# A transformer pass on one core: each feed-forward network computed in three parts, each part followed by its share of the down projection

## The chip, the cores and the metric

The kernel runs on one core of a Trainium2 chip, whose other cores are idle. The metric is the time of one execution in device microseconds. TensorE multiplies, VectorE (DVE), ScalarE (ACT) and GpSimd (POOL) work on whole tiles of 128 partitions by 512 elements, and SyncE (SP) issues the transfers from HBM. Every engine runs its own program in order, and a semaphore is what makes one wait for another.

## What is computed

One sequence of 512 tokens of width 1024 passes through a mixer block, a memory attention, two more mixers and five feed-forward networks (FFN 0 to 4), each with 2816 hidden channels. The change concerns the five networks. In the reference they are these two functions (the first is FFN 0, the second FFN 1 to 4), and the lines around FFN 0:

```python
def conv_ffn(n, w_up, conv_w, conv_b, w_down):
    u, g = jnp.split(n @ w_up, 2, axis=-1)
    ...
    gc = sum(gp[:, j:j + S] * conv_w[j] for j in range(CONV_WIDTH)) + conv_b
    return (jax.nn.silu(gc) * u) @ w_down
...
def swiglu(x, w_gate, w_up, w_down):
    return (jax.nn.silu(x @ w_gate) * (x @ w_up)) @ w_down
...
        n = rms_norm(h, norm_ffn[l])
        h = h + conv_ffn(n, w_up[l], conv_w[l], conv_b[l], w_down[l])
    return rms_norm(h, final_norm)
```

After FFN 0 the residual is normed twice in a row: `final_norm` ends the first block, and the norm of FFN 1 follows at once.

## The kernel before

**Data.** The residual `h` lies transposed in SBUF as 8 tiles (`KT`) of 128 channels by 512 tokens. All matrix products are in three passes: an operand is split in a rounded part and a rest (`_hi` and `_lo`, type fp32r), and `products` (L1793 to L1795) adds w_hi·x_hi, w_hi·x_lo and w_lo·x_hi into one PSUM bank.

**Weights.** They come from HBM as one stream of 248 chunks of 1 MB, in the order of use. A chunk goes to one of two `stage` buffers by a transfer on SP's queue; ACT makes `w_hi` of it (`split_hi`, L450), DVE `w_lo` (`split_lo`, L901), each in one of two buffers. `split_hi` of a chunk waits until PE has finished the chunk two before (`chunk_done`); PE waits for `lo_ready`. A chunk holds 8 k-tiles by 2 output tiles, so 48 products of 128x512; the two output tiles take 2 of 4 PSUM banks, which alternate, so the next but one chunk needs them evacuated (`acc_evac`).

**An FFN** has two stages. `up` has 22 chunks, in pairs: a gate chunk and an up chunk, each of 2 of the 22 hidden tiles. DVE evacuates the gate (L947; for FFN 0 followed by the convolution), ACT takes the SiLU, DVE evacuates the up product (L964), POOL multiplies them (L1672), ACT rounds the result into `f_hi` (L497), DVE writes the rest `f_lo` (L968). All 22 tiles are kept: `f_hi` and `f_lo` hold 22 tiles each. `down` has 12 chunks: for each of 4 pairs of output tiles the 22 hidden tiles in chunks of 8, 8 and 6, which accumulate in the same two PSUM banks. The third chunk of each three is padded in HBM, and PE works 36 products on it.

**The residual** stage (`residual`) belongs to the end of each `down`: per pair of output tiles DVE adds the PSUM banks to `h` (L926), then splits the next chunk's weights (L901), and writes `x_lo` of the two tiles (L932) behind ACT's `x_hi` (L469). POOL follows with `sums`: per tile it squares `h` into `sq` (L1648) and adds that to `ssum` (L1650). PE sums `ssum` over the partitions by a product with ones (`stat`, L1833) after the first chunk of the next stage, ACT takes the root, DVE the reciprocal, and that `rstd` is needed for the evacuation of that first chunk.

**After FFN 0** a second sum is formed for the double norm: ACT writes the weighted squares to `sq_b` (L473), POOL adds them to `both_sum`, which lies in `up_b` (L1656), for both tiles of a pair, and only then does it square and sum the two tiles as above. PE's product with `both_sum` (`both`, L1838) stands after the first chunk of FFN 1's `up` stage. The plain sum is used for `final_norm` itself: PE's `stat(3)` stands after all of `up` of FFN 1, then ACT and DVE make the factor, and POOL multiplies the 8 tiles of `h` by the gain (L1720) and by the factor (L1724) before the down projection is added.

In all these stages the loops are hardware loops (`walk`), with two chunks, or the chunks of two pairs of output tiles, in a turn.

Of the kernel before, what the change touches and what calls it, by code (L numbers as in the profile page):

```python
# [19 lines left out]
F32 = mybir.dt.float32  # L20
# [28 lines left out]

PHASES = [  # L50
    ("qf", 6, 12), ("v", 2, 4), ("gla", 12, 24), ("kv_a", 1, 2), ("merge", 4, 16), ("mix_out", 4, 8),
    ("mem_k", 4, 8), ("mem_v", 4, 8), ("mem_q", 4, 8), ("mem_o", 4, 8),
    ("up0", 22, 44), ("down0", 12, 8),
    ("up1", 22, 44), ("down1", 12, 8),
    ("a_in", 5, 10), ("mla", 3, 20), ("a_out", 4, 8),
    ("up2", 22, 44), ("down2", 12, 8),
    ("up3", 22, 44), ("down3", 12, 8),
    ("c_in", 12, 24), ("c_out", 4, 8),
    ("up4", 22, 44), ("down4", 12, 8),
# [57 lines left out]
def build(nc, stream, x_in, mem_in, pos_in, par_in, const_in, out):  # L117
    ctx = ExitStack()
    with ctx:
# [42 lines left out]
        f_hi = place("f_hi", HID, [P, FT, S], F32R)  # L162
        f_lo = place("f_lo", hid(FT), [P, FT, S], F32R)
# [103 lines left out]
        def sem(name):  # L267
# [24 lines left out]
        qf_act, f_ready1, g_ready = sem("qf_act"), sem("f_ready1"), sem("g_ready")  # L292
# [4 lines left out]
        const_landed, wa_const_ready, kv_done, rot_step = (  # L297
            sem("const_landed"), sem("wa_const_ready"), sem("kv_done"), sem("rot_step"))
# [8 lines left out]
        mem_landed, mem_sq_ready, mem_stat, mem_std, mem_n, mem_hi_ready, mem_ready = (  # L307
            sem("mem_landed"), sem("mem_sq_ready"), sem("mem_stat"), sem("mem_std"), sem("mem_n"), sem("mem_hi_ready"), sem("mem_ready"))
# [6 lines left out]
        rope2_landed, lat_sq, lat_stat, lat_std, lat_recip, lat_n, lat_hi_ready, lat_ready = (  # L315
            sem("rope2_landed"), sem("lat_sq"), sem("lat_stat"), sem("lat_std"), sem("lat_recip"), sem("lat_n"), sem("lat_hi_ready"), sem("lat_ready"))
        pool_scaled = sem("pool_scaled")
        u_pad, pool_step, pl_hi_ready, pl_ready, mla_tile, cat0_hi, cat0_ready = (
            sem("u_pad"), sem("pool_step"), sem("pl_hi_ready"), sem("pl_ready"), sem("mla_tile"), sem("cat0_hi"), sem("cat0_ready"))
        mla_const, t5_ready, kr_sum, kr_copied = sem("mla_const"), sem("t5_ready"), sem("kr_sum"), sem("kr_copied")  # L320
# [7 lines left out]
        cu_pad, cu_ready, cv_step, cz_ready, cc_hi_ready, cc_ready = (  # L328
            sem("cu_pad"), sem("cu_ready"), sem("cv_step"), sem("cz_ready"), sem("cc_hi_ready"), sem("cc_ready"))
# [10 lines left out]
        UPS = {f"up{i}": i for i in range(5)}  # L340
# [6 lines left out]
        for name in RESIDUALS:  # L347
            XR0[name] = KT + _n
            _n += KT if FOLLOWED[name] else 0

# [88 lines left out]
        def _(act):  # L439
# [16 lines left out]
            def residual(name):  # L456
                r0, t0, c0 = XR0[name], T0[name], C0[name]
                gain = FOLLOWED[name]
                per = 6 if name.startswith("down") else 2

                def step(it):
                    for pair in range(2):
                        for k in range(per // 2):
                            split_hi((c0 + 2 + pair * (per // 2) + k, it * per))
# [17 lines left out]
            def up(name):  # L482
                c0, t0, f0, conv = C0[name], T0[name], FT * UPS[name], name == "up0"

                def step(it):
                    split_hi((c0 + 2, it * 2))
                    for e in range(2):
                        if conv:
                            act.wait_ge(conv_step, it * 6 + 3 * e + 3)
                            act.activation(gate_b[:, e, 1:1 + S], up_b[:, e, :], ACT.Silu).then_inc(silu_ready, 1)  # L490
                        else:
                            act.wait_ge(acc_evac, it * 4 + t0 + e + 1)
                            act.activation(gate_b[:, e, 1:1 + S], gate_b[:, e, 1:1 + S], ACT.Silu).then_inc(silu_ready, 1)
                    split_hi((c0 + 3, it * 2))
                    for e in range(2):
                        act.wait_ge(prod_ready, it * 2 + f0 + e + 1)
                        act.activation(row(f_hi, it * 2 + e), up_b[:, e, :], ACT.Copy).then_inc(f_hi_ready, 1)  # L497
# [2114 lines left out]
```

## Time and profile before

| what | value |
|---|---|
| time, median of 3 runs | 2785.27 us (2784.6 to 2785.38) |
| the profiled execution, from first to last instruction | 2783.7 us |
| PE busy | 2765.9 us, 99% |
| PE weight load busy | 2293.1 us, 82% |
| DVE, ACT, POOL busy | 1427.2, 1006.1, 509.2 us (51%, 36%, 18%) |
| granted TensorE clock | 1.000 over the span |
| mean DMA rate | 95 GB/s |

The page gives the profiled execution by its span alone, 2783.7 us; what a run's time has beside it is the 1.6 us by which the median is higher. Busy time of PE is an account of records that overlap: a product is shown 0.39 us long, and the next starts before it has ended, so the distance from start to start is what tells how fast PE works.

### The profile page before, as it was taken

The page shows a single profiled execution, that of the slowest core. Times are in us where ns is not written, and L with a number is a line of the kernel's source. Part 1 is how long each engine was busy: PE and PEld are TensorE (multiplying, and loading weights), DVE is VectorE, ACT ScalarE, POOL GpSimd, SP SyncE. Part 2 cuts the span into 40 slices and gives each one's busy share as a digit, 9 for nine tenths or more (in the row PEclk, how much of TensorE's full clock was granted, in tenths as well). Part 3 has the DMA queues.
Part 4 walks back from the last instruction along what each step waited for, and adds up shares of the span by engine and source line. Part 5 has one row for each costly group of instructions (what it writes and reads, how often), then busy time and mean ns, then how long its engine had stood idle before and what let it go on. Part 6 is the DMA issues. An engine that isn't in the chain of part 4 may idle for free.

```text
span 2783.7 us, 33669 instructions
## 1 busy us (share of the span) xinstructions
PE 2765.9 (99%) x12836; PEld 2293.1 (82%) x12836; DVE 1427.2 (51%) x1392; ACT 1006.1 (36%) x1099; POOL 509.2 (18%) x364
## 2 busy tenths in 40 slices
PE   9999999999999999999999999999999999999999
PEld 7978889878888888888778888888888888888887
DVE  5778766566654444343575444334443455644422
ACT  4333633434432344332263444324443222344421
POOL 0124013041101310052123100121110222501100
PEclk9999999999999999999999999999999999999999
DMA  4212024223222322323212222232223322232232
GB/s 165 90 62 79 31 106 148 79 76 106 91 105 95 115 92 90 105 91 105 99 35 74 104 91 97 99 106 104 92 90 106 106 98 99 91 105 91 90 106 91
DMA packets 39676, 264.97 MB, mean 95 GB/s; under 512 B 4528, under 2 KB 5808, under 8 KB 8240
## 3 DMA queue, kind: packets, MB, share of 16 engines
q1 hardware_dynamic: 38016, 259.02, 26.8%
q10 hardware_dynamic: 1584, 4.87, 0.5%
q8 instruction: 56, 0.92, 0.1%
q14 instruction: 20, 0.16, 0.0%
HBM read 261.77 MB, written 2.10 MB: 95 GB/s over the span
## 4 chain that ended last, share of the span: by engine, by line
PE 96%; DVE 2%; ACT 1%; issue 0%; DMA 0%; SPq 0%; POOL 0%; DVEq 0%; POOLq 0%; ACTq 0%
PE ps L1793 30%; PE ps L1794 30%; PE ps L1795 30%; PE ps L1956 1%; PE ps L2022 1%; PE ps L2053 1%; PE ps L2347 1%; PE ps L2319 1%; PE ps L1978 1%; DVE w_lo L901 0%; PE ps L2036 0%; PE ps L2331 0%; ACT w_hi L450 0%; DMA stage<-in_stream 0%; PE ps L1833 0%
## 5 line engine op out<-in xcount | busy, mean ns | idle before, releaser
L450 ACT ACTIVATE w_hi<-stage 128x2048 fp32r<-128x2048 f32 x241 | 462.8, 1920 | 1354.3 <-PE ps L1795 1351.8
L1793 PE MATMUL ps<-x_hi,w_hi 128*128 128x512 f32 x2400 | 943.3, 393 | 2.2 <-DVE w_lo L977 2.0
L1795 PE MATMUL ps<-x_hi,w_lo 128*128 128x512 f32 x2400 | 934.0, 389 | 0.0
L1794 PE MATMUL ps<-x_lo,w_hi 128*128 128x512 f32 x2400 | 933.9, 389 | 0.0
L901 DVE TENSOR_TENSOR w_lo<-stage,w_hi 128x2048 fp32r<-128x2048 f32 x241 | 602.1, 2498 | 397.1 <-ACT w_hi L450 397.1
L1793 PEld LDWEIGHTS ps<-x_hi,w_hi 128*128 128x128 f32 x2400 | 450.6, 188 | 98.9 <-issue 3.5
L1794 PEld LDWEIGHTS ps<-x_lo,w_hi 128*128 128x128 f32 x2400 | 450.7, 188 | 95.4 <-issue 3.4
L1795 PEld LDWEIGHTS ps<-x_hi,w_lo 128*128 128x128 f32 x2400 | 450.5, 188 | 93.9
L1793 PE MATMUL ps<-f_hi,w_hi 128*128 128x512 f32 x880 | 342.7, 389 | 0.0
L1794 PE MATMUL ps<-f_lo,w_hi 128*128 128x512 f32 x880 | 342.3, 389 | 0.0
L1795 PE MATMUL ps<-f_hi,w_lo 128*128 128x512 f32 x880 | 342.3, 389 | 0.0
L1672 POOL TENSOR_TENSOR up_b<-up_b,gate_b 128x512 f32<-128x512 f32 x110 | 118.1, 1094 | 1050.9 <-DVE up_b L964 1034.8
L964 DVE TENSOR_TENSOR up_b<-ps,rstd 128x512 f32<-128x512 f32 x110 | 71.0, 687 | 299.1 <-PE ps L1795 299.0
L1793 PEld LDWEIGHTS ps<-f_hi,w_hi 128*128 128x128 f32 x880 | 165.2, 188 | 34.7 <-issue 0.2
L1795 PEld LDWEIGHTS ps<-f_hi,w_lo 128*128 128x128 f32 x880 | 165.2, 188 | 34.3
L1794 PEld LDWEIGHTS ps<-f_lo,w_hi 128*128 128x128 f32 x880 | 165.2, 188 | 34.3 <-issue 0.2
L947 DVE TENSOR_TENSOR gate_b<-ps,rstd 128x512 f32<-128x512 f32 x110 | 71.0, 688 | 230.2 <-PE ps L1795 229.2
L1648 POOL TENSOR_TENSOR sq<-h 128x512 f32 x64 | 80.6, 1259 | 500.1 <-DVE h L926 494.1
L1650 POOL TENSOR_TENSOR ssum<-ssum,sq 128x512 f32<-128x512 f32 x64 | 140.0, 2187 | 5.0
L926 DVE SCALAR_TENSOR_TENSOR h<-ps,h 128x512 f32 (+1 forms) x72 | 46.4, 686 | 131.2 <-PE ps L1795 127.1
L932 DVE SCALAR_TENSOR_TENSOR x_lo<-h,par,x_hi x64 | 104.2, 1666 | 0.0
L497 ACT ACTIVATE f_hi<-up_b 128x512 f32 x110 | 69.8, 635 | 26.7 <-POOL up_b L1672 23.1
(401 smaller groups left out, 2616.3 us busy)
## 6 DMA issues: line engine op xcount, KB each, us to landing
stage<-in_stream SPq DMA_DIRECT2D x242, 1024.0 KB, 4.9
h<-in_x ACTq DMA_DIRECT2D x2, 1024.0 KB, 5.7
out_x<-h SPq DMA_DIRECT2D x8, 256.0 KB, 6.0
h<-in_x SPq DMA_DIRECT2D x6, 256.0 KB, 4.4
mem_raw<-in_mem ACTq DMA_DIRECT2D x1, 1024.0 KB, 4.8
stage<-in_stream SPq DMA_DIRECT2D x6, 128.0 KB, 5.0
h<-in_x SPq DMA_DIRECT2D x1, 512.0 KB, 5.4
mask_f<-in_constants ACTq DMA_DIRECT2D x1, 448.0 KB, 6.3
```

The source lines that it names most:

```text
L450: act.activation(w_hi[slot][:, :], stage[slot][:, :], ACT.Copy).then_inc(hi_ready, 1)
L497: act.activation(row(f_hi, it * 2 + e), up_b[:, e, :], ACT.Copy).then_inc(f_hi_ready, 1)
L901: dve.tensor_tensor(w_lo[slot][:, :], stage[slot][:, :], w_hi[slot][:, :].bitcast(F32), ALU.subtract).then_inc(lo_ready, 1)
L932: dve.scalar_tensor_tensor(row(x_lo, it * 4 + m), row(h, it * 4 + m), pc(gain, it * 4 + m), row(x_hi, it * 4 + m).bitcast(F32), ALU.mult, ...
L947: dve.tensor_tensor(gate_b[:, e, 1:1 + S], ps[:, (t0 + e) % 4, :], rstd[:, :], ALU.mult).then_inc(acc_evac, 1)
L964: dve.tensor_tensor(up_b[:, e, :], ps[:, (t0 + 2 + e) % 4, :], rstd[:, :], ALU.mult).then_inc(acc_evac, 1)
L1648: pool.tensor_tensor(sq[:, :], row(h, m), row(h, m), ALU.mult).then_inc(sq_ready, 1)
L1650: pool.tensor_tensor(ssum[:, :], ssum[:, :], sq[:, :], ALU.add).then_inc(ss_ready, 1)
L1672: pool.tensor_tensor(up_b[:, e, :], up_b[:, e, :], gate_b[:, e, 1:1 + S], ALU.mult).then_inc(prod_ready, 1)
L1793: pe.matmul(out_ap, wh, xh, start=first, stop=False)
L1794: pe.matmul(out_ap, wh, xl, start=False, stop=False)
L1795: return pe.matmul(out_ap, wl, xh, start=False, stop=last)
```

## The change

Each FFN is cut in three parts: hidden tiles 0 to 7, 8 to 15 and 16 to 21 (`PARTS`: 4, 4 and 3 pairs of up chunks). After the up chunks of a part come 4 down chunks, one for each pair of output tiles, with 8, 8 or 6 k-tiles. Each down chunk now ends in an evacuation: for parts a and b DVE adds it to `h` straight away, and part c is followed by the `residual` stage as before, now with one chunk to a pair of output tiles. `f_hi` and `f_lo` shrink to 8 tiles each. The chunks stay 248 and the products as many; the padded chunks stand together at the end. Up stages and the down stages are written out instead of looped. For FFN 1, `h` has to be scaled before the first part is added: `stat(3)`, the root, the reciprocal and POOL's 16 instructions move into the second, third and fourth step of the up stage. Some semaphores are merged to save their number; these waits are the same in meaning.

```diff
+KP = KT // 2
+PARTS = [("a", 0, 4), ("b", 4, 4), ("c", 8, 3)]
+STEPS = FT // 2
...
-        f_hi = place("f_hi", HID, [P, FT, S], F32R)
-        f_lo = place("f_lo", hid(FT), [P, FT, S], F32R)
+        f_hi = place("f_hi", HID, [P, 8, S], F32R)
+        f_lo = place("f_lo", hid(8), [P, 8, S], F32R)
...
# vector engine, residual stage (per is now 2 everywhere)
-                        for k in range(per // 2 - 1):
-                            dve.wait_ge(chunk_done, it * per + (c0 + pair * (per // 2) + k + 1))
-                            split_lo((c0 + 2 + pair * (per // 2) + k, it * per))
-                        dve.wait_ge(chunk_done, it * per + (last + 1))
+                        dve.wait_ge(chunk_done, it * 2 + (c0 + pair + 1))
...
+            def ffn(i):
...
+                        if i == 1 and it == 1:
+                            dve.wait_ge(std_ready, NS0["renorm"] + 1)
+                            dve.reciprocal(sq[:, :], ssum[:, :]).then_inc(rstd_ready, 1)
+                    if part != "c":
+                        c, t = C0[_down_name(i, part)], T0[_down_name(i, part)]
+                        for j in range(4):
+                            dve.wait_ge(chunk_done, c + j + 1)
+                            for e in range(2):
+                                m = 2 * j + e
+                                if i == 1 and part == "a":
+                                    dve.wait_ge(renormed, KT + m + 1)
+                                dve.scalar_tensor_tensor(h[:, m, :], ps[:, (t + m) % 4, :], scale, h[:, m, :], ALU.mult, ALU.add).then_inc(acc_evac, 1)
+                            split_lo((c + j + 2, 0))
...
# GpSimd
+            def ffn(i):
+
+                for it in range(STEPS):
+                    _, t = gate_chunk(i, it)
+                    for e in range(2):
+                        pool.wait_ge(silu_ready, FT * i + 2 * it + e + 1)
+                        pool.wait_ge(acc_evac, t + 2 + e + 1)
+                        pool.tensor_tensor(up_b[:, e, :], up_b[:, e, :], gate_b[:, e, 1:1 + S], ALU.mult).then_inc(prod_ready, 1)
+                    if i == 1 and it == 1:
+                        pool.wait_ge(x_ready, XR0["down0"] + KT)
+                        for m in range(KT):
+                            pool.tensor_scalar(h[:, m, :], h[:, m, :], pc("final_norm", m), None, ALU.mult).then_inc(renormed, 1)
+                        pool.wait_ge(rstd_ready, NS0["renorm"] + 1)
+                    if i == 1 and it in (2, 3):
+                        for m in range(KP * (it - 2), KP * (it - 1)):
+                            pool.wait_ge(renormed, KT + m)
+                            pool.tensor_tensor(h[:, m, :], h[:, m, :], sq[:, :], ALU.mult).then_inc(renormed, 1)
...
# TensorE
+            def ffn(i, of, before):
+
+                for part, base, count in PARTS:
+                    for it in range(base, base + count):
+                        c, t = gate_chunk(i, it)
+                        plain(c, t, x, (x_ready, XR0[of]) if it == 0 else None)
+                        if it == 0:
+                            before()
+                        if i == 1 and it == 1:
+                            stat(3)
+                        plain(c + 1, t + 2, x)
+                    c, t = C0[_down_name(i, part)], T0[_down_name(i, part)]
+                    for j in range(4):
+                        begin(c + j, t + 2 * j, 2)
+                        for k in range(2 * count):
                             if j == 0:
+                                pe.wait_ge(f_ready, past(FT * i + 2 * base + k + 1))
                             for m in range(2):
+                                mm = products(ps[:, (t + 2 * j + m) % 4, :], w_at(c + j, k * PAIR + m * P, P),
+                                              (f_hi[:, k, :], f_lo[:, k, :]), k == 0, k == 2 * count - 1)
                         mm.then_inc(chunk_done, 1)
```

**Where rows move: DVE at the end of FFN 0.** These are DVE's rows for one pair of output tiles of `down0`; `w_lo` is the split of a weight chunk, `h` the addition to the residual, `x_lo` the rest part for the next stage. Before:

```order
L900 REGISTER_ALU [waits chunk_done]
L901 TENSOR_TENSOR w_lo_57<-stage_53,w_hi_55 128x2048 [waits hi_ready]
L918 REGISTER_ALU
L900 REGISTER_ALU [waits chunk_done]
L901 TENSOR_TENSOR w_lo_56<-stage_52,w_hi_54 128x2048 [waits hi_ready]
L926 ISA [waits chunk_done]
L926 SCALAR_TENSOR_TENSOR h<-ps,h 128x512
L926 ISA
L926 SCALAR_TENSOR_TENSOR h<-ps,h 128x512
L900 REGISTER_ALU
L901 TENSOR_TENSOR w_lo_57<-stage_53,w_hi_55 128x2048 [waits hi_ready]
L931 REGISTER_ALU
```

After, the same place (the last of the three parts):

```order
L948 ISA [waits chunk_done]
L948 SCALAR_TENSOR_TENSOR h<-ps,h 128x512
L948 ISA
L948 SCALAR_TENSOR_TENSOR h<-ps,h 128x512
L922 REGISTER_ALU
L923 TENSOR_TENSOR w_lo_57<-stage_53,w_hi_55 128x2048 [waits hi_ready]
L953 REGISTER_ALU
L954 ISA [waits x_hi_ready]
L954 SCALAR_TENSOR_TENSOR x_lo<-h,par,x_hi 128x512
```

Two weight splits with a wait for a chunk each are gone from between two pairs: the additions to `h` of one pair and of the next are now one chunk apart instead of three.

**PE at the end of the first down chunk of a part.** `f_hi` and `f_lo` are the hidden tiles, `w_hi` and `w_lo` the weights. Before, after the eighth of 22 hidden tiles:

```order
L1793 MATMUL ps<-f_hi,w_hi_55 128x512 [waits f_ready]
L1794 MATMUL ps<-f_lo,w_hi_55 128x512
L1795 MATMUL ps<-f_hi,w_lo_57 128x512
L1793 MATMUL ps<-f_hi,w_hi_55 128x512
L1794 MATMUL ps<-f_lo,w_hi_55 128x512
L1795 MATMUL ps<-f_hi,w_lo_57 128x512
L1867 REGISTER_ALU
L1793 MATMUL ps<-f_hi,w_hi_54 128x512 [waits f_ready,lo_ready]
```

After, in the third part, after the sixth and last of its hidden tiles:

```order
L1826 MATMUL ps<-f_hi,w_hi_55 128x512 [waits f_ready]
L1827 MATMUL ps<-f_lo,w_hi_55 128x512
L1828 MATMUL ps<-f_hi,w_lo_57 128x512
L1826 MATMUL ps<-f_hi,w_hi_55 128x512
L1827 MATMUL ps<-f_lo,w_hi_55 128x512
L1828 MATMUL ps<-f_hi,w_lo_57 128x512
L1826 MATMUL ps<-f_hi,w_hi_54 128x512 [waits acc_evac,lo_ready]
```

The newest hidden tile, which used to be the 22nd in line, is now the sixth, and the next chunk goes to other banks.

**POOL around FFN 1.** Before, `up` in a loop of two products, and all 16 scalings of `h` behind it:

```order
L1672 TENSOR_TENSOR up_b<-up_b,gate_b 128x512 [waits acc_evac]
L404 REGISTER_ALU
L404 COMPARE_AND_BRANCH
L1720 ISA
L1720 TENSOR_SCALAR h<-h,par 128x512 x8
L1724 TENSOR_TENSOR h<-h,sq 128x512 [waits renormed,rstd_ready]
L1724 TENSOR_TENSOR h<-h,sq 128x512 [waits renormed] x7
```

After:

```order
L1704 TENSOR_TENSOR up_b<-up_b,gate_b 128x512 [waits acc_evac,silu_ready] x4
L1708 ISA
L1708 TENSOR_SCALAR h<-h,par 128x512 [waits x_ready]
L1708 TENSOR_SCALAR h<-h,par 128x512 x7
L1704 TENSOR_TENSOR up_b<-up_b,gate_b 128x512 [waits acc_evac,silu_ready,rstd_ready]
L1704 TENSOR_TENSOR up_b<-up_b,gate_b 128x512 [waits acc_evac,silu_ready]
L1713 TENSOR_TENSOR h<-h,sq 128x512 [waits renormed] x4
L1704 TENSOR_TENSOR up_b<-up_b,gate_b 128x512 [waits acc_evac,silu_ready] x2
L1713 TENSOR_TENSOR h<-h,sq 128x512 [waits renormed] x4
```

The scalings now stand between the products of FFN 1's second, third and fourth steps.

## Rows read from the trace of the kernel before

**Rows 1.** The chain of waits, and PE's row of the page

```profile
PE 96%; DVE 2%; ACT 1%; issue 0%; DMA 0%; SPq 0%; POOL 0%; DVEq 0%; POOLq 0%; ACTq 0%
...
PE 2765.9 (99%) x12836; PEld 2293.1 (82%) x12836; DVE 1427.2 (51%) x1392; ACT 1006.1 (36%) x1099; POOL 509.2 (18%) x364
```

**Rows 2.** Windows on FFN 0 and 2: length, PE, PEld, DVE, ACT, POOL busy, clock

```profile
617.00:977.00 360.00, 360.00 (x1587) 297.67 (x1586) 193.13 (x183) 133.05 (x118) 58.51 (x48) 1.00 0.29 99
1536.00:1896.00 360.00, 360.00 (x1588) 297.72 (x1587) 149.65 (x117) 127.15 (x110) 52.64 (x39) 1.00 0.29 99
```

**Rows 3.** Timeline of PE in the up stage: start, length

```profile
978.82 0.39 PE L1793 MATMUL ps<-x_hi,w_hi 128*128 128x512 f32 x1
979.50 0.39 PE L1793 MATMUL ps<-x_hi,w_hi 128*128 128x512 f32 x1
```

**Rows 4.** Timeline of PE and DVE, FFN 0 from up to down

```profile
846.03 0.39 PE L1793 MATMUL ps<-f_hi,w_hi 128*128 128x512 f32 x1
...
848.19 3.11 DVE L901 TENSOR_TENSOR w_lo<-stage,w_hi 128x2048 fp32r<-128x2048 f32 x1 [0.67 <-ACT w_hi L450]
851.22 1.28 DVE L968 TENSOR_TENSOR f_lo<-up_b,f_hi 128x512 f32 x2
```

**Rows 5.** Timeline of DVE and PE where PE waits for a weight split

```profile
581.53 2.32 DVE L901 TENSOR_TENSOR w_lo<-stage,w_hi 128x2048 fp32r<-128x2048 f32 x1 [0.53 <-ACT w_hi L450]
...
583.91 0.50 PE L1793 MATMUL ps<-mo_hi,w_hi 128*128 128x512 f32 x1 [1.65 <-DVE w_lo L901]
584.24 0.40 PE L1794 MATMUL ps<-mo_lo,w_hi 128*128 128x512 f32 x1
```

**Rows 6.** Timeline of PE, last pair of down0 and FFN 1's first chunk

```profile
965.71 0.39 PE L1793 MATMUL ps<-x_hi,w_hi 128*128 128x512 f32 x1
...
976.59 1.02 PE L1838 MATMUL ps<-up_b,const 128*128 128x512 f32 x2
```

**Rows 7.** Timeline of DVE and POOL there

```profile
966.04 1.29 DVE L926 SCALAR_TENSOR_TENSOR h<-ps,h 128x512 f32 x2 [4.05 <-PE ps L1795]
967.86 2.29 DVE L901 TENSOR_TENSOR w_lo<-stage,w_hi 128x2048 fp32r<-128x2048 f32 x1 [0.53 <-ACT w_hi L450]
970.07 3.49 DVE L932 SCALAR_TENSOR_TENSOR x_lo<-h,par,x_hi  x2
...
969.21 3.80 POOL L1656 TENSOR_TENSOR up_b<-up_b,sq_b 128x512 f32<-128x512 f32 x2 [20.70 <-ACT sq_b L473]
972.97 1.49 POOL L1648 TENSOR_TENSOR sq<-h 128x512 f32 x1
974.54 1.29 POOL L1650 TENSOR_TENSOR ssum<-ssum,sq 128x512 f32<-128x512 f32 x1
976.01 1.04 POOL L1648 TENSOR_TENSOR sq<-h 128x512 f32 x1 [0.18 <-POOL ssum L1650]
977.13 1.29 POOL L1650 TENSOR_TENSOR ssum<-ssum,sq 128x512 f32<-128x512 f32 x1
```

**Rows 8.** Timeline of POOL and PE, last pair of c_out before FFN 4

```profile
2421.05 1.04 POOL L1648 TENSOR_TENSOR sq<-h 128x512 f32 x1 [3.40 <-DVE h L926]
2422.16 3.22 POOL L1650 TENSOR_TENSOR ssum<-ssum,sq 128x512 f32<-128x512 f32 x1
2425.57 1.26 POOL L1648 TENSOR_TENSOR sq<-h 128x512 f32 x1 [0.19 <-POOL ssum L1650]
2426.91 1.61 POOL L1650 TENSOR_TENSOR ssum<-ssum,sq 128x512 f32<-128x512 f32 x1
...
2430.64 1.02 PE L1833 MATMUL ps<-ssum,const 128*128 128x512 f32 x2
```

**Rows 9.** Critical chain at the start: DVE's x_lo with POOL idle

```profile
15.23 1.42 DVE x_lo L985 x2
```

**Rows 10.** Timeline of POOL in FFN 1, the eight scalings of h

```profile
1209.11 16.01 POOL L1720 TENSOR_SCALAR h<-h,par 128x512 f32<-128x512 f32 x8
```

**Rows 11.** DMA queues: packets, MB, share of 16 engines

```profile
q8 instruction: 56, 0.92, 0.1%
```

More of the change, by code:

```diff
@@ L47, with _down_name, _ffn @@
 PAIR = 256
+KP = KT // 2
+PARTS = [("a", 0, 4), ("b", 4, 4), ("c", 8, 3)]
+STEPS = FT // 2
+def _down_name(i, part):
+    return f"down{i}" if part == "c" else f"down{i}{part}"
+def _ffn(i):
+    return [phase for part, _, n in PARTS for phase in ((f"up{i}{part}", 2 * n, 4 * n), (_down_name(i, part), 4, 8))]
 PHASES = [
@@ L458, in residual @@
                 gain = FOLLOWED[name]
-                per = 6 if name.startswith("down") else 2
                 def step(it):
                     for pair in range(2):
-                        for k in range(per // 2):
-                            split_hi((c0 + 2 + pair * (per // 2) + k, it * per))
+                        split_hi((c0 + 2 + pair, it * 2))
                         for e in range(2):
@@ L480, in residual, with rounded @@
                     walk(act, 2, step)
[L482 to L497, printed above, removed]
-                walk(act, FT // 2, step)
+            def ffn(i):
+                def rounded(it, e):
+                    act.wait_ge(prod_ready, FT * i + 2 * it + e + 1)
+                    act.activation(f_hi[:, 2 * it % 8 + e, :], up_b[:, e, :], ACT.Copy).then_inc(f_hi_ready, 1)
+                for part, base, count in PARTS:
+                    end = base + count
+                    for it in range(base, end):
+                        c, t = gate_chunk(i, it)
+                        if i == 1 and it == 1:
+                            stat(NS0["renorm"])
+                        split_hi((c + 2, 0))
+                        for e in range(2):
+                            if i == 0:
+                                act.wait_ge(conv_step, 6 * it + 3 * e + 3)
+                                act.activation(gate_b[:, e, 1:1 + S], up_b[:, e, :], ACT.Silu).then_inc(silu_ready, 1)
+                            else:
+                                act.wait_ge(acc_evac, t + e + 1)
+                                act.activation(gate_b[:, e, 1:1 + S], gate_b[:, e, 1:1 + S], ACT.Silu).then_inc(silu_ready, 1)
+                        split_hi((c + 3, 0))
+                        rounded(it, 0)
+                        rounded(it, 1)
+                    if part != "c":
+                        c = C0[_down_name(i, part)]
+                        for j in range(4):
+                            split_hi((c + j + 2, 0))
@@ L1417, in _ @@
             dve.wait_ge(rstd_ready, NS0["down0"] + 1)
[L1418 to L1420 removed]
+            ffn(1)
             residual("down1")
@@ L2196, in _ @@
             walk(pe, 2, out_step, 1)
-            linear("up0", x, (x_ready, XR0["mem_o"]), before=2)
-            down("down0")
-            linear("up1", x, (x_ready, XR0["down0"]), before=both)
-            stat(3)
-            down("down1")
+            ffn(0, "mem_o", lambda: stat(2))
+            ffn(1, "down0", both)
             c, t = C0["a_in"], T0["a_in"]
@@ L2395, in _ @@
                 some(c + i, t + 2 * i, range(KT), cat)
-            linear("up2", x, (x_ready, XR0["a_out"]), before=5)
-            down("down2")
-            linear("up3", x, (x_ready, XR0["down2"]), before=6)
-            down("down3")
+            ffn(2, "a_out", lambda: stat(5))
+            ffn(3, "down2", lambda: stat(6))
             c3, t3 = C0["c_in"], T0["c_in"]
@@ L2413, in _ @@
             linear("c_out", (cc_hi, cc_lo), (cc_ready, 0))
-            linear("up4", x, (x_ready, XR0["c_out"]), before=8)
-            down("down4")
+            ffn(4, "c_out", lambda: stat(8))
 def _cols(w, cols):
```

276 lines of the change are left out of this document (124 added, 152 removed).

## The prediction

> **What bounds the kernel now.** I read the chain of waits first: PE holds 96% of it, and PE is shown busy for 99% of the span [rows 1]. Other engines set the time only where PE waits for them. Then I ask how close PE is to its own pace. In the timeline of the up stage the third product after one starts 0.68 us later, so they are 0.2267 us apart [rows 3]; a chunk of 48 takes 10.88 us, a down chunk of 6 k-tiles (36 products) 8.16 us. FFN 0 has 1584 products: 359.1 us at that pace. Its window is full of PE for 360.0 us [rows 2], and the sum product that stands in every stage (1.02 us, [rows 6]) accounts for the rest. The same stands for FFN 2. So loop turns, semaphores and transfers cost PE nothing there: what the change removes on any other engine can give nothing back, and only two things can move the time: a wait of PE that is new, and PE's own stream of instructions.
>
> **What is removed or added at no cost.** The products stay 12836 and the chunks 248. Unrolling removes PE's branches; by [rows 2] they take under 0.1 us in an FFN, so I book 0, at most 0.5 us for all five. DVE gets 16 more additions to `h` for each FFN, half of 1.29 us each [rows 7], 80 x 0.65 = 52 us on an engine that is idle for half of the span. What they might delay is the split of the weights behind them: in the residual stage, where addition and split already stand in this order, the split ends 967.86 + 2.29 - 965.71 = 4.4 us after the chunk [rows 6, 7], and PE wants it 8.16 or 10.88 us after it. If this cover went, each late microsecond would be PE's. In front of FFN 0, 2, 3 and 4 nothing else moves.
>
> For FFN 1 the scaling of `h` moves forward. `stat(3)` costs PE what it cost before. POOL's eight scalings take 16.0 us [rows 10] and begin some 3 us after the second step's last chunk; the next product of POOL is due 21.8 us after it, so they end about 2.6 us ahead of it. If they were late, it would delay hidden tiles that PE reads only after two more steps: 0 again. The 8 further multiplications go in two groups of four behind the third and fourth steps, and the first additions that need them come a down chunk later.
>
> **The first term: the newest hidden tiles.** Before, the last two of 22 hidden tiles were read after 20 others. Now they are the last two of 8, or of 6. After the last up chunk the down stage starts at 846.03, and DVE writes the two `f_lo` from 851.22 in 1.28 us [rows 4]; the first is there after half of that, 5.87 us behind PE's start. PE follows the end of a DVE instruction by 0.06 us, and its next product comes after 0.33 us instead of 0.227: 0.1 us lost at a restart [rows 5]. In parts a and b the tile is wanted after 6 k-tiles, 36 x 0.2267 = 8.16 us: hidden. In part c it is wanted after 4, 24 x 0.2267 = 5.44 us, and is there at 5.93: a wait of 0.49 + 0.10 = 0.6 us. The second tile (6.5 us) is in time. Five networks: 3.0 us. Bounds: the split ahead of `f_lo` takes 3.11 us there and 2.29 when POOL is quiet [rows 4, 7]; 0.8 us earlier would leave nothing, and at most as much later 1.4 us each. I take 3.0, since every operation up to `f_lo` stays as it is.
>
> **The second term: POOL's two sums behind FFN 0.** Here the pace of the pairs changes. Before, pairs of output tiles ended 30 us apart; now in part c 8.16 us. For an ordinary sum POOL needs 2428.52 - 2421.05 = 7.5 us for a pair [rows 8], with DVE's work beside it, so it keeps up, and the last sum is there 2.1 us before PE's product with it at 2430.64. That margin stays for down1, down2 and down3.
>
> After FFN 0 POOL has two more additions in each pair. From [rows 7] one tile's square and sum take 2.4 us plus 0.18 between; free of DVE a pair costs 2 x 2.6 + 2 x 1.4 = 8.0 us, just under 8.16. But POOL and DVE get in each other's way: an addition of 1.29 us takes 3.22 when DVE splits weights beside it [rows 8], and DVE's two `x_lo`, 1.42 us with POOL quiet [rows 9], take 3.49 [rows 7]. DVE has in each chunk one split (2.3) and two `x_lo` (1.4), 3.7 us in which POOL mostly stands. So a pair costs between 8.0 and 11.7 us, and POOL falls behind. I walked both queues, granting one instruction with two SBUF operands at a time to whoever asks first; it gives the ordinary pair 7.7 us where the row has 7.5. Counted from the end of pair 1's chunk (965.71 in the present rows), POOL begins the first additions at 3.5, as now, those of pairs 2, 3 and 4 at 15.4, 26.3 and 36.9, and ends the last at 39.4. PE comes to its product with `both_sum` after three more down chunks and one up chunk: 3 x 8.16 + 10.88 = 35.4 us. It waits 4.0 us and loses 0.1 at the restart. Bounds: at 8.0 us a pair there is no wait; at 11.7 the last addition ends at 3.5 + 35.1 + 2.8 = 41.4, a wait of 6.0. I take 4.1 from the walk, since in the last ten microseconds DVE has nothing to do.
>
> Behind that product everything stands as before, shifted. Behind PE's wait stands only the up chunk of the same step; DVE and ACT wait for the reciprocal anyway. The last `x_lo` of FFN 0 is late too, at 33.0 us by the walk, but PE wants its tile at 24.5 + 7 x 1.36 = 34.0.
>
> The Trainium skill (SBUF — State Buffer, the rules on who interferes with whom) calls the pair of ports that DVE and GpSimd share an exclusive lock, held for a whole instruction. By it the full serial price would hold, 6.0 us of wait and 2794.4 us in all. The ordinary pair of [rows 8] agrees in kind but costs 7.5 us, less than its 5.2 free plus 3.7: not all of DVE's time is lost to POOL.
>
> **Sum.** 3.0 + 4.1 = 7.1 us: from the span 2783.7 to 2790.8, and from the median 2785.3 to 2792.4 us, 0.25% more. What a measurement of this kernel can tell from no change is about 0.2%, 5.6 us.
>
> **Rivals.**
> *POOL keeps up* (not slower by 0.2%). If POOL slips its work into DVE's gaps, a pair costs near 8.2 us, the wait at `both_sum` is under 2.5 us, and the time 2785.3 + 3.0 + 0 to 2.4 = 2788.3 to 2790.7. For it: the free price of 8.0 is under 8.16. Against: 3.22 against 1.29 us. It decides below a pair of 9.9 us or so. 0.20.
> *The clock falls.* PE's granted clock is 1.00 throughout [rows 2], but its waits now are 1.65 us at most in the full flow [rows 5]; one of 4 is new. A chunk at 1.2 GHz would take up to 10.9 us more; a part of one to a whole one gives 2795 to 2803. 0.12. The Trainium skill (TensorE: Matmul & The Clock Gate, Part 1) says that idleness halves the clock until PE has been busy again; no run here shows it yet.
> *The stream of instructions gets slow.* PE's program grows from 6188 rows to 11738. It fetched 56 blocks with 0.92 MB [rows 11] without a visible gap, and written-out stages run today; some microseconds more if this fails. 0.04.
> *No effect, or faster.* Both waits hidden, or loop turns worth more than rows show: 2785 or just below. 0.04, of which faster 0.03. The Trainium skill (Runtime: NRT & Kernel Launch, Instruction fetch mechanics) holds that a taken branch outside of the fetched pages costs a stall, so that unrolling pays. At 360.0 us for an FFN with some thirteen turns [rows 2] there is nothing to win.
>
> **Numbers.** The forecast itself has 0.60, its own range 2790 to 2795; of it 0.03 lies within 0.2%. Slower: 0.57 + 0.12 + 0.04 = 0.73. Within 0.2%: 0.03 + 0.20 + 0.01 = 0.24. Faster: 0.03. The range runs from 2787.5, below POOL keeping up, to 2797, both upper bounds or a short stretch of slow clock.
>
> **What would show it.** PE waits at the product with `up_b` for POOL, 4 us, once; PE waits five times near 0.6 us for `f_lo`, each 24 products into the third part; nowhere else more than before; products still 0.2267 us apart. POOL's additions into `up_b` in pairs 11 us apart. I am wrong if the wait at `both_sum` is under 2.5 us or over 6, if DVE's splits come late in the 8.16 us chunks, or if the clock leaves 1.00.

## The result, and the profile after

The changed kernel takes 2793.04 us in the median of 9 runs (2790.84 to 2794.14), the kernel before, on the same chip, 2785.27 (2784.60 to 2785.78, 9 runs): a ratio of 1.0027, 95% interval [1.0017, 1.0037]. It is slower: the interval lies above 1, and begins just under the 0.2% that the prediction asked for. The profiled execution took 2791.3 us, its span is 2789.5, which is 5.8 us over the span before.

The page of the changed kernel, engines, DMA queue of instructions and chain of waits, as in [rows 1, 11]:

```profile
PE 2767.5 (99%) x12836; PEld 2292.6 (82%) x12836; DVE 1487.5 (53%) x1472; ACT 867.6 (31%) x996; POOL 518.2 (19%) x364
...
q8 instruction: 100, 1.64, 0.2%
...
PE 94%; DVE 2%; ACT 1%; issue 1%; POOL 1%; DMA 0%; SPq 0%; DVEq 0%; POOLq 0%; ACTq 0%
```

The products are as many, PE is busy 1.6 us more, DVE 60 us more (52 were booked), ACT 139 us less (the first experiment says why); POOL has entered the chain with 1%. The page says that something waits, not what. PE's waits of the changed kernel by line and releaser (us in total, times, longest) say it:

```profile
PE ps L1871 <- POOL up_b L1688: 2.9, 1, 2.9
PE ps L1826 <- DVE f_lo L992: 2.2, 5, 0.5
```

Neither row exists before; the others are those of before, apart from waits for weight splits in the first microseconds of the kernel. The first is the product with `both_sum` behind FFN 0, once; the second is `f_lo`, once in each network. Timeline of PE at both places in FFN 0 (start, length, in brackets the idle time and who ended it):

```profile
937.02 0.39 PE L1828 MATMUL ps<-f_hi,w_lo 128*128 128x512 f32 x1
937.79 0.50 PE L1826 MATMUL ps<-f_hi,w_hi 128*128 128x512 f32 x1 [0.38 <-DVE f_lo L992]
938.13 0.40 PE L1827 MATMUL ps<-f_lo,w_hi 128*128 128x512 f32 x1
...
975.82 0.39 PE L1828 MATMUL ps<-x_hi,w_lo 128*128 128x512 f32 x1
979.11 1.13 PE L1871 MATMUL ps<-up_b,const 128*128 128x512 f32 x2 [2.90 <-POOL up_b L1688]
979.67 0.80 PE L1826 MATMUL ps<-x_hi,w_hi 128*128 128x512 f32 x1
980.31 0.40 PE L1827 MATMUL ps<-x_lo,w_hi 128*128 128x512 f32 x1
```

The bracket is shorter than the loss, because a modelled end stands in it. What is lost is read from starts, as in the prediction: 937.79 - 937.02 - 0.227 = 0.54 us, and 0.11 at the product behind it, 0.34 instead of 0.227; at `both_sum` 979.11 - 975.82 - 0.227 = 3.06 us, and 0.1 behind it.

Since every trace has the same 12836 products in nearly the same order, the loss can be placed without any row of waits: the start of product number n in the one trace less that of the same number in the other. I count from product 3001, since the two traces differ by 1.3 us before it in how long the first weights take to arrive, which is no part of the change. The growth of this difference against the kernel before:

```
                      FFN 0 f_lo  both_sum  FFN 1  FFN 2  FFN 3  FFN 4   to the last product
changed kernel             0.77      3.19   0.80   0.77   0.78   0.79   7.11
```

It grows at these six places. Elsewhere only 0.4 us appear at 1002 us and are gone again by 1210, in FFN 1: the change moves the sum product of `stat(3)` to the first of these places, and before it stood at the second. The change costs 7.1 us: 3.9 at `f_lo`, 3.2 at `both_sum`.

POOL and DVE behind FFN 0's last part in the changed kernel, which answer to [rows 7]:

```profile
944.18 3.80 POOL L1688 TENSOR_TENSOR up_b<-up_b,sq_b 128x512 f32<-128x512 f32 x2 [5.22 <-ACT sq_b L488]
...
952.11 3.22 POOL L1682 TENSOR_TENSOR ssum<-ssum,sq 128x512 f32<-128x512 f32 x1
955.29 3.44 POOL L1688 TENSOR_TENSOR up_b<-up_b,sq_b 128x512 f32<-128x512 f32 x2
...
966.14 4.62 POOL L1688 TENSOR_TENSOR up_b<-up_b,sq_b 128x512 f32<-128x512 f32 x2
...
976.45 2.60 POOL L1688 TENSOR_TENSOR up_b<-up_b,sq_b 128x512 f32<-128x512 f32 x2
...
951.00 3.18 DVE L923 TENSOR_TENSOR w_lo<-stage,w_hi 128x2048 fp32r<-128x2048 f32 x1 [0.54 <-ACT w_hi L467]
954.10 3.48 DVE L954 SCALAR_TENSOR_TENSOR x_lo<-h,par,x_hi  x2
```

Only the first pair of additions has idle time ahead of it; behind it POOL works without a pause of more than 0.18 us, and still falls behind. PE begins the chunk after pair 1 at 940.69. Counted from there the four pairs of additions begin at 3.5, 14.6, 25.5 and 35.8 and the last ends at 38.4 (the hand walk had 3.5, 15.4, 26.3, 36.9 and 39.4). Two sums and two additions cost 11.1, 10.9 and 10.3 us for a pair, while PE brings one every 8.16.

### The profile page after: what moved, and what is told of

Read it like the earlier page. It is cut to its first block, busy times and chain, and to the rows that moved or that the text cites. A ratio compares the mean times of both kernels' runs of the same rounds, so it can differ in the third digit from the quotient of the medians.

```text
span 2789.5 us, 31953 instructions
## 1 busy us (share of the span) xinstructions
PE 2767.5 (99%) x12836; PEld 2292.6 (82%) x12836; DVE 1487.5 (53%) x1472; ACT 867.6 (31%) x996; POOL 518.2 (19%) x364
## 4 chain that ended last, share of the span: by engine, by line
PE 94%; DVE 2%; ACT 1%; issue 1%; POOL 1%; DMA 0%; SPq 0%; DVEq 0%; POOLq 0%; ACTq 0%
PE ps L1826 30%; PE ps L1828 29%; PE ps L1827 29%; PE ps L1986 1%; DVE w_lo L923 1%; PE ps L2052 1%; PE ps L2083 1%; ACT w_hi L467 1%; PE ps L2374 1%; PE ps L2346 1%; PE ps L2008 1%; PE ps L2066 0%; PE ps L2358 0%; PE ps L1866 0%; DMA stage<-in_stream 0%
## 5 line engine op out<-in xcount | busy, mean ns | idle before, releaser
L1704 POOL TENSOR_TENSOR up_b<-up_b,gate_b 128x512 f32<-128x512 f32 x110 | 120.3, 1115 | 1449.7 <-DVE up_b L987 1434.1
L1004 DVE SCALAR_TENSOR_TENSOR h<-ps,h 128x512 f32<-128x512 f32 x80 | 51.5, 686 | 240.1 <-PE ps L1828 240.1
L1682 POOL TENSOR_TENSOR ssum<-ssum,sq 128x512 f32<-128x512 f32 x64 | 146.4, 2288 | 5.0
```

Of the source, the lines that this page charges most:

```text
L1004: dve.scalar_tensor_tensor(h[:, m, :], ps[:, (t + m) % 4, :], scale, h[:, m, :], ALU.mult, ALU.add).then_inc(acc_evac, 1)
L1682: pool.tensor_tensor(ssum[:, :], ssum[:, :], sq[:, :], ALU.add).then_inc(ss_ready, 1)
L1704: pool.tensor_tensor(up_b[:, e, :], up_b[:, e, :], gate_b[:, e, 1:1 + S], ALU.mult).then_inc(prod_ready, 1)
```

## The experiments

They stand in the order in which they were run. Times of the kernel before are those of the same chip. The growth from product 3001 to the last, as above, is called the trace's difference to the kernel before.

**Unrolling alone.** The kernel before, with the loops over the steps of the up stages written out on PE, ACT, DVE and POOL, and those of the down stages on PE.

```diff
-                walk(dve, FT // 2, step)
+                for it in range(FT // 2):
+                    step(it)
```

> The kernel before, with the loops of the up and down stages of PE and the up stages of ACT, DVE and POOL written out, nothing else. Theory of the waits (the 7.8 us of the change are two new kinds of wait of PE, plus what the clock makes of one of them): no new wait, span 2783.7 within 0.3, time 2785.3, runs as close together as those of the kernel before (1 us). Rival, the stream of instructions: the written-out program is what costs, and what makes the runs of the changed kernel differ by 3 us; then the time is 2 to 5 us above 2785.3 and the runs spread. If taken branches cost something, the time falls below 2784.5.

2784.41 us (2784.19 to 2784.93, 11 runs), before 2784.49 (33 runs): ratio 0.9999 [0.9990, 1.0008]. The trace's difference is 0.00 us, and PE's longest waits are those of before. Written-out code costs nothing, and loop turns gave nothing back; the 7.1 us belong to the thirds.

This kernel also says where ACT's 139 us went, which the thirds have no part in. ACT's busy time is 864.8 us here, as low as in the changed kernel. Before, ACT loads an activation table (`ACT_TABLE_LOAD`) 131 times, here 26 times and in the changed kernel 28 times, 1.28 us each. 110 of the 131 stand in the 55 turns of the up loop, two in each turn. Two of these groups, the first before, the second here at the SiLU of FFN 1 to 4, which has 44 loads before:

```profile
L450 ACT ACT_TABLE_LOAD x55 | 70.6, 1283 | 1.0
L493 ACT ACT_TABLE_LOAD x4 | 5.1, 1283 | 0.1
```

With PE's starts unchanged to 0.00 us, their going is worth nothing here.

**POOL's additions ahead.** In the changed kernel POOL does the two additions into `both_sum` of a pair before its own two sums of the pair ahead of it.

```diff
-                    for e in range(2):
-                        own(it * 2 + e)
...
+                    for it in range(1, KT // 2):
+                        adds(it)
+                        own(2 * it - 2)
+                        own(2 * it - 1)
```

> The changed kernel; behind FFN 0 POOL makes the two additions to both_sum of a pair before the squares and plain sums of the pair ahead of it, so these are one pair late. Same operations. Theory of the waits: the wait of 2.9 us at the product with both_sum goes, the five at f_lo stay; span 2789.5 - 3.1 = 2786.4. The granted clock was given as 0.999 in the seven slower runs of the changed kernel and 1.000 in the two fastest; theory of the clock: this wait is what lowers it, so without it every run shows 1.000 and the time is 2788.1 with runs within 1 us, 5 us under the median of 2793.0. Rival: the spread has another source (written-out code, transfers); then the time is 2788 to 2791 and runs still differ by 3 us.

2789.20 us (2788.79 to 2789.57, 11 runs): ratio 1.0017 [1.0008, 1.0026]. The trace's difference falls from 7.11 to 4.89 us. PE's waits in this kernel's trace:

```profile
PE ps L1830 <- DVE f_lo L992: 2.2, 5, 0.5
PE ps L1875 <- POOL up_b L1688: 0.8, 1, 0.8
```

I had the wait at `both_sum` gone: 1.1 us of its 3.2 stay. The reason stands in the edit: the squares and plain sums of pair 2 still stand between the additions of pair 3 and those of pair 4, and POOL is behind by then. POOL's additions for pairs 3 and 4 in this kernel's trace, 10.85 us apart:

```profile
963.70 3.44 POOL L1688 TENSOR_TENSOR up_b<-up_b,sq_b 128x512 f32<-128x512 f32 x2
...
974.55 2.70 POOL L1688 TENSOR_TENSOR up_b<-up_b,sq_b 128x512 f32<-128x512 f32 x2
```

The distance of the medians to the kernel before fell further than the trace says, from 7.8 to 4.7 us, by 3.1 where the trace has 2.2; the two waits alone don't explain that.

**The rest first.** In the changed kernel the last up step of each network lets DVE write `f_lo` before the split of the weights, which is not needed as soon.

```diff
-                        split_lo((c + 3, 0))
+                        if it < STEPS - 1:
+                            split_lo((c + 3, 0))
                         for e in range(2):
...
+                        if it == STEPS - 1:
+                            split_lo((c + 3, 0))
```

> The changed kernel; in the last step of each network's up stage DVE writes f_lo of the two hidden tiles before it splits the next weight chunk, not behind it. Theory of the waits: f_lo is there 2 us earlier, the five waits of 0.5 us go, no other comes (the split ends some 7 us after the chunk, wanted at 8.2): span 2789.5 - 2.7 = 2786.8. Theory of the clock: the longer wait stays, so most runs still show 0.999 and spread over 3 us, median 2790.3. Rival: the split is now late and PE waits for it instead, span 2789 or more.

2789.09 us (2787.03 to 2790.24, 11 runs): ratio 1.0014 [1.0005, 1.0023]. No wait for `f_lo` is left in any network, so the 3.9 us are that wait and nothing else of the thirds. But the trace's difference is 4.97 us where 3.2 should be left. Timeline of PE in this trace:

```profile
978.78 1.13 PE L1874 MATMUL ps<-up_b,const 128*128 128x512 f32 x2 [3.11 <-POOL up_b L1691]
...
980.01 0.63 PE L1830 MATMUL ps<-x_lo,w_hi 128*128 128x512 f32 x1
980.44 0.63 PE L1831 MATMUL ps<-x_hi,w_lo 128*128 128x512 f32 x1
980.87 0.63 PE L1829 MATMUL ps<-x_hi,w_hi 128*128 128x512 f32 x1
...
983.38 0.39 PE L1829 MATMUL ps<-x_hi,w_hi 128*128 128x512 f32 x1
983.62 0.39 PE L1830 MATMUL ps<-x_lo,w_hi 128*128 128x512 f32 x1
```

Behind the wait of 3.11 us eight products stand 0.43 us apart and not 0.227: 8 x 0.2 = 1.6 us. The granted clock says the same. Windows of this kernel's trace (length, busy time of PE, PEld, DVE, ACT and POOL, granted clock, DMA share, GB/s):

```profile
964.00:976.00 12.00, 11.67 (x52) 9.33 (x50) 7.68 (x6) 5.80 (x6) 11.51 (x8) 1.00 0.41 155
976.00:984.00 8.00, 5.22 (x14) 3.84 (x15) 3.33 (x1) 3.77 (x3) 7.26 (x7) 0.79 0.00 0
984.00:992.00 8.00, 8.00 (x37) 6.61 (x36) 3.50 (x4) 1.23 (x2) 0.00 (x0) 1.00 0.38 131
```

0.79 over 8 us is 3.4 us at the lower of the clock's two levels, 1.2 GHz. The sum product itself still has the 1.13 us that it has in the changed kernel: the granted clock is 1.00 from 978.80 to 979.80, with PE at work again, and 0.50 from 980.00 to 983.00, so it fell about 1 us after the wait had ended. The mean clock of the whole run is 0.998 or 0.999 in 8 of this kernel's 11 runs, whose spans are 1 to 3 us longer than those of the 3 with 1.000. The same stands for the changed kernel: 7 of its 9 runs have 0.999 and take 2792.82 to 2794.14 us; the two at 1.000 take 2790.84 and 2791.3, and the profiled one is of these. That is the rival of the falling clock, and it came on top of the forecast. It fits the steeper fall of the median in the kernel before this: all 11 runs there, with 0.8 us of wait left, are at 1.000.

**Both.** Additions ahead and rest first together.

> Both edits at once. Theory of the waits with that of the clock: nothing of the loss is left, span 2783.7 within 0.4, time 2785.3, runs within 1 us, clock 1.000. Rival: if something in the three parts beside these two waits costs time (16 more additions for a network, the moved scalings), the time stays 1 us or more above 2785.3.

2785.41 us (2784.95 to 2786.20, 11 runs): ratio 1.0003 [0.9994, 1.0012], every run at a clock of 1.000. The trace's difference is 1.13 us, all of it the 0.8 us wait at `both_sum` with its restart. The two terms add up: 7.11 less the 3.9 of `f_lo` and less the 2.2 that the additions ahead gave is 1.0.

**A longer wait, twice.** To see whether the clock's price grows with the wait: the changed kernel with 5, and with 14, memsets of a spare tile on POOL ahead of the last pair's additions.

```diff
+                    if it == KT // 2 - 1:
+                        for q in range(5):
+                            pool.memset(idle_t[:, q, :], 0.0)
```

> The changed kernel with five memsets of an unused tile (0.5 us each) on POOL ahead of the last pair's additions to both_sum, and POOL's loop over the pairs written out: one wait is lengthened, from 2.9 to 5.5 us. Theory of the clock (the wait lowers PE's clock, and a fixed stretch at 1.2 GHz follows, 1.6 us lost in the trace of the kernel with f_lo first): now every run shows a granted clock of 0.999 or less, and the time is the kernel before plus 3.6 (f_lo) plus 5.8 (wait) plus 1.6 to 2: 11.0 to 11.5 us over it, with runs closer together than the 3 us of the changed kernel. Rival: the clock's cost grows with the length of the wait, or runs still differ by 3 us.

> The same with fourteen memsets: a wait of 10.3 us. Theory of the clock: the loss through the clock stays 1.6 to 2 us, so 15.8 to 16.3 us over the kernel before. Rival (the cost grows with the wait, as if PE took longer to come back after a longer rest): more than 18 us over it.

With 5: 2796.16 us (2795.29 to 2796.55, 5 runs), before 2785.36 (21 runs), ratio 1.0038 [1.0025, 1.0052]. With 14: 2800.28 (2799.39 to 2800.32, 5 runs), ratio 1.0053 [1.0039, 1.0066]. The traces' differences are 12.27 and 16.38 us. Timeline of PE with 5:

```profile
981.23 2.07 PE L1876 MATMUL ps<-up_b,const 128*128 128x512 f32 x2 [5.25 <-POOL up_b L1692]
982.31 1.41 PE L1831 MATMUL ps<-x_hi,w_hi 128*128 128x512 f32 x1
983.52 0.63 PE L1832 MATMUL ps<-x_lo,w_hi 128*128 128x512 f32 x1
...
987.37 0.42 PE L1832 MATMUL ps<-x_lo,w_hi 128*128 128x512 f32 x1
987.62 0.39 PE L1833 MATMUL ps<-x_hi,w_lo 128*128 128x512 f32 x1
```

and with 14:

```profile
985.41 2.08 PE L1876 MATMUL ps<-up_b,const 128*128 128x512 f32 x2 [9.45 <-POOL up_b L1692]
986.50 1.42 PE L1831 MATMUL ps<-x_hi,w_hi 128*128 128x512 f32 x1
987.71 0.63 PE L1832 MATMUL ps<-x_lo,w_hi 128*128 128x512 f32 x1
...
991.13 0.56 PE L1831 MATMUL ps<-x_hi,w_hi 128*128 128x512 f32 x1
991.52 0.40 PE L1832 MATMUL ps<-x_lo,w_hi 128*128 128x512 f32 x1
```

Nine products 0.43 us apart in both, the sum product itself twice as long (2.07 against 1.13 us), and then full speed: the clock costs 2.8 to 2.9 us beside the wait, whether PE stood for 5 or for 9.5 us. All ten runs have a clock of 0.998 or 0.999.

Both forecasts missed in their parts. The waits are shorter than foretold (5.2 and 9.5 us for 5.5 and 10.3), and the clock's price is higher (2.8 to 2.9 us for 1.6 to 2), since here the clock fell while PE still stood and the sum product fell into the slow stretch as well. The medians, 10.8 and 14.9 us over the kernel before, lie under the foretold ranges of 11.0 to 11.5 and 15.8 to 16.3, the traces' differences above them. The rival of a price that grows on with the wait, over 18 us for the second kernel, is refuted.

So the clock is a charge that hardly changes between 5 and 9.5 us of wait. It was there in all 10 runs at 5 us and more, in 15 of 20 at 3 us, and in none of 32 behind 0.7 to 0.8 us (the kernels additions ahead, both, and the last one below). Once it fell without such a wait: of the 67 runs of the kernel before whose clock is on record one has 0.999, and takes 2787.99 us where the median of its 21 is 2785.36. No trace of that run was kept.

**Parts of 3, 4 and 4 steps.** The changed kernel with the short part first, so that the last part is as long as the second. The indices follow, and the eight multiplications of `h` for FFN 1 stand in one group behind the third step.

```diff
-PARTS = [("a", 0, 4), ("b", 4, 4), ("c", 8, 3)]
+PARTS = [("a", 0, 3), ("b", 3, 4), ("c", 7, 4)]
```

> The changed kernel with the short part in front: parts of 3, 4 and 4 pairs of up chunks, in FFN 1 all eight multiplications of h behind the third step. The pairs of output tiles of down0 are now 10.9 us apart, not 8.16. Theory of the pace (POOL needs 10.3 to 11.1 us for a pair): the wait at both_sum is gone, and with it the clock's part; the f_lo wait moves to the first part and stays 0.73 us in each network: 3.6 us over the kernel before, runs within 1.5 us. Rival: POOL's pairs take as much longer as the chunks do (it is DVE's work that it waits for, not its own that is too long), and 2 us or more of wait stay.

2789.66 us (2788.92 to 2790.44, 11 runs), ratio 1.0016 [1.0007, 1.0025], the clock at 1.000 in all; the trace's difference is 5.26 us where 3.6 were foretold. The wait at `both_sum` is gone: a down chunk of the last part now has 8 k-tiles, 48 products, 10.88 us, and POOL's pairs of additions begin 10.88 us apart. The wait for `f_lo` has only moved to the new short part, and in FFN 1 it grew, which was not foretold. Timeline of DVE, POOL and PE there, in this kernel's trace:

```profile
1033.94 3.22 DVE L923 TENSOR_TENSOR w_lo<-stage,w_hi 128x2048 fp32r<-128x2048 f32 x1 [0.65 <-ACT w_hi L467]
1037.09 3.45 DVE L992 TENSOR_TENSOR f_lo<-up_b,f_hi 128x512 fp32r<-128x512 f32 x2
...
1034.97 8.11 POOL L1713 TENSOR_TENSOR h<-h,sq 128x512 f32<-128x512 f32 x4
...
1038.89 0.50 PE L1826 MATMUL ps<-f_hi,w_hi 128*128 128x512 f32 x1 [1.56 <-DVE f_lo L992]
```

POOL's multiplications of `h` for FFN 1 fall on the moment when DVE writes `f_lo`, which takes 3.45 us for two tiles and not 1.28; POOL's four take 8.11 us where four of its ordinary multiplications, 1115 ns in the page's mean, would take 4.5. FFN 1 costs 2.2 us here, each other network 0.74 to 0.79.

**All sums last.** Both repairs, and POOL's additions of the last two pairs ahead of the own sums of pairs 2 to 4.

```diff
-                    for it in range(1, KT // 2):
-                        adds(it)
-                        own(2 * it - 2)
-                        own(2 * it - 1)
-                    own(KT - 2)
-                    own(KT - 1)
+                    adds(1)
+                    own(0)
+                    own(1)
+                    adds(2)
+                    adds(3)
+                    for m in range(2, KT):
+                        own(m)
```

> Both mended, with the additions of the last two pairs both ahead of the squares and plain sums of pairs 2 to 4: the wait at both_sum that was left with them one pair late was 1.0 us. Theory of the waits: nothing is left, the time is that of the kernel before within 0.3 us. Rival: 0.9 us stay, then it is the three parts themselves.

2784.40 us (2783.91 to 2784.70, 11 runs), ratio 0.9996 [0.9987, 1.0005]; the trace's difference is 0.03 us. With three changes of order the thirds cost nothing, and they gain nothing either: this is the floor that PE's own pace sets. No version is faster than the kernel before, clear of noise.

**One operand.** What makes POOL slow is still argued from coincidence in time, so DVE's work beside it was changed.

```diff
-                            if gain:
+                            if name == "down0":
+                                dve.wait_ge(x_hi_ready, it * 4 + (r0 + m + 1))
+                                dve.tensor_scalar(row(x_lo, it * 4 + m), row(h, it * 4 + m), pc(gain, it * 4 + m),
+                                                  0.001, ALU.mult, ALU.mult).then_inc(x_ready, 1)
+                            elif gain:
```

> The changed kernel, but at the end of FFN 0's first part (after down0) DVE writes x_lo from h alone, with one operand (h times gain times 0.001), where it subtracted x_hi from h times gain; so x_lo's values differ, and nothing else is changed. It asks whether DVE's two-operand work slows POOL's sums and additions, and with that makes the wait at both_sum. Theory (DVE and POOL share a way to SBUF, and an operation with one operand takes it less): POOL's sums and additions beside x_lo come nearer to their durations alone, POOL's last addition ends up to 4 us earlier, the wait at both_sum of 2.9 us goes to 0 to 1 us, the rest stays: 2.3 to 3.2 us less than the changed kernel, about 2790 us, every run with the clock at 1.000. Rival (POOL's queue is simply that long, or the one-operand form disturbs it as much): POOL's durations stay, the wait stays 2.5 to 3.3 us, about 2793 us.

2789.11 us (2788.64 to 2789.53, 10 runs), before 2784.43 (13 runs; both on another chip than the runs of the experiments above), ratio 1.0016 [1.0007, 1.0026], the clock at 1.000 in all ten. The waits for `f_lo` stay at 2.2 us, the one at `both_sum` falls from 2.9 to 0.7 us; the trace's difference is 4.82 us, 2.3 less than for the changed kernel. POOL's and DVE's rows of this kernel beside each other:

```profile
955.14 2.91 POOL L1692 TENSOR_TENSOR up_b<-up_b,sq_b 128x512 f32<-128x512 f32 x2
...
964.87 2.85 POOL L1692 TENSOR_TENSOR up_b<-up_b,sq_b 128x512 f32<-128x512 f32 x2
...
953.96 2.95 DVE L954 TENSOR_SCALAR x_lo<-h,par  x2
...
959.54 3.04 DVE L923 TENSOR_TENSOR w_lo<-stage,w_hi 128x2048 fp32r<-128x2048 f32 x1 [0.55 <-ACT w_hi L467]
```

The additions of pairs 2 and 3 take 2.9 us where they took 3.44, against 2.60 with DVE idle, and POOL's pairs come 10.6, 9.7 and 9.8 us apart where they came 11.1, 10.9 and 10.3. No instruction of POOL was touched, so the contention with DVE is shown to set the pace of its queue.

The one-operand form is not free of it either. DVE's two `x_lo` take 2.95 us, 1.5 us each, with POOL at work beside them. With POOL idle a `tensor_scalar` on a tile of the same size, in the convolution of FFN 0, takes 0.54 us (this kernel's row for that line: shortest, median and longest of 22, in ns), and the two-operand `x_lo` 1.42 us for two [rows 9]:

```profile
L982 DVE TENSOR_SCALAR up_b<-gate_b,par x22: 539/542/543, 624.4 to 928.1; 128x512 f32<-128x512 f32 x22
```

So DVE is slowed in this form too, while POOL suffers less from it. The two `tensor_scalar` still differ in the type of their output and in one factor, a constant in `x_lo`; no row has the very form of `x_lo` with POOL idle. The output type alone is not slow: the two-operand `x_lo` writes the same type. The splits of the weights still collide with POOL as before.

## Why the prediction was right, and where its parts were not

- **The bound.** PE's own pace sets the time and nothing on another engine could be given back: right. The last repair comes out at 0.03 us from the kernel before, and 139 us less of ACT, the table loads, bought nothing.
- **Unrolling at no cost:** right, 0.00 us measured. The Trainium skill (Runtime: NRT & Kernel Launch, Instruction fetch mechanics) would have had unrolling pay; neither that nor the rival of a slow instruction stream showed, with 100 blocks of instructions fetched instead of 56.
- **The first term, `f_lo`:** five waits at the foretold product, right in mechanism and place, under-sized: 3.0 foretold, 3.9 measured. In FFN 0 the tile came 5.93 us behind PE's start in the down stage (931.81 to the row above at 937.79, less 0.06), as foretold. In the other four it came at about 6.0. (Half of 1.28 us behind 851.22 would be 5.83 us behind PE's start, where the prediction writes 5.87; it changes the term by 0.2 us.) The step that was off is "0.1 us lost at a restart" with nothing behind it: each restart costs 0.11, the first wait is 0.54 and the others 0.62 us, and some products behind it stand 0.24 and not 0.227 us apart.
- **The second term, `both_sum`:** right in mechanism and place, over-sized: 4.1 foretold, 3.2 measured. The walk had POOL and DVE take turns instruction by instruction, and was 0.8 us late from the second pair on, 1.0 at the end. That the sum fits, 7.1 foretold and 7.11 measured from the traces, is luck: the two errors, 0.9 us too little and 0.9 too much, cancel.
- **A rule that was weighed.** The exclusive lock of the Trainium skill (SBUF — State Buffer, Who interferes with whom), with all of DVE's work taken to fall on POOL's, would have given a wait of 6.0 us; it was 2.9. Rows and last experiment agree with it in kind: both engines are slowed, POOL up to 3.22 against 1.29 us. A pair costs 10.3 to 11.1 us and not the full serial price of 11.7.
- **The rival of the falling clock** had 0.12, and it came true in 7 of 9 runs. Its price was the mistake: not 3 to 11 us, but 1.6 to 2.9, since the clock returns after eight or nine products. In the changed kernel, whose profiled run shows none of it, the runs with the lower clock are 1.5 to 3.3 us longer than the other two. The rule of the Trainium skill (TensorE: Matmul & The Clock Gate, Part 1) that idleness halves the clock until PE has been busy again is borne out in the three traces with waits of 3.1, 5.2 and 9.5 us, though not in the changed kernel's with 2.9. The sentence "I am wrong if the clock leaves 1.00" applies to the seven runs, though not to the profiled one.
- **The median.** 2793.0 for 2792.4 looks closer than it is. The sum of terms holds no clock, so its forecast is for the two runs at 1.000, and these take 2790.84 and 2791.3, 1.3 us less: in its trace the kernel before gets its first weights later by that much, which the count from product 3001 leaves out. With the other seven, which the clock made longer, the median comes 2 us higher. That it falls so near the forecast is luck too.
- **POOL keeps up** (0.20) was refuted, if not by much. Its limit of 9.9 us for a pair does not follow from the prediction's own terms: 3.5 + 3 x 10.5 + 2.8 less 35.4 is 2.4, so the wait stays under its 2.5 us up to a pair of 10.5. The three measured pairs are 10.8 in the mean, and the wait was 2.9.
- The splits of DVE in the 8.16 us chunks were never late, and FFN 1's moved scalings cost nothing, as booked. With another cut of the parts the multiplications of FFN 1 do cost 1.4 us, so that zero was a matter of place.

What stays open: why the clock falls in 15 of 20 runs behind the same wait of 3 us and not in the other 5, and why it fell in one run of the kernel before. Between 1 and 2.9 us of wait the runs show only that waits of 1.1 to 1.65 us, which stand in every kernel here, go with a clock of 1.000 in nearly all runs.

## What to carry to other kernels

When a long stage is cut into short ones, the work doesn't grow, but every producer's last result gets a shorter cover. List, for each operand of the first product of each short stage, when it is ready behind the stage's start, and compare with the new cover, not with the old. A helper engine that was idle between pairs 30 us apart can be the bound when they come 8 us apart: take its price per pair with its neighbour's work beside it, not from rows where it runs alone. And before a cut is thrown away, try the order of instructions in the helpers' queues, since on DVE and POOL that alone returned all 7.1 us here.

## What the runs showed of the hardware that was not expected

- The clock of PE fell to its lower level behind a single wait of about 3 us between long stretches at full work, in 15 of 20 runs of two kernels, never (32 runs) behind 0.7 to 0.8 us; it also fell in 1 of 67 runs of the kernel before, whose longest wait in the full flow is 1.65 us. After 3.1 us of wait the record fell about 1 us after PE had gone on; in the run with 9.5 us at 981.2, while PE still stood.
- The price rises from 1.6 us after 3.1 us of wait to 2.9 after 5.2, and not further: 2.8 after 9.5.
- A product of this kernel takes 0.227 us from start to start at the full clock and 0.43 us at half: 1.9 times, not 2.
- DVE's one-operand `x_lo` takes 1.3 to 1.5 us with POOL at work beside it, where a one-operand instruction of the same size takes 0.54 us with POOL idle.
- ACT loaded its activation table twice in each turn of the up loop, 1.28 us a time: 131 loads, and 26 with the same steps written out.
